# Two transformer blocks on one core: where sigmoids, up-tile copies, PSUM banks and sums of squares are placed

## Time and profile before

| | |
|---|---|
| time, median of three runs | 955.78 us (955.57 to 955.84) |
| the profiled execution: its time, its span | 955.88 us, 954.7 us |
| TensorE matmul, weight load busy | 926.0 us (97%), 887.9 us (93%) |
| VectorE, ScalarE, GpSimd busy | 664.5 us (70%), 480.2 us (50%), 68.3 us (7%) |
| DMA | 154.73 MB, mean 162 GB/s |
| instructions recorded | 17976, of which 7290 matmuls |

### The profile page before, as it was taken

How to read it: one execution, slowest core, us unless ns; L and a number is a source line. 1 busy time by engine, 2 the same in 40 slices (tenths; PEclk the granted TensorE clock), 3 DMA queues, 4 the chain that set the end, 5 groups by cost and what they waited for, 6 DMA issues and landing times.

```text
span 954.7 us, 17976 instructions
## 1 busy us (share of the span) xinstructions
PE 926.0 (97%) x7290; PEld 887.9 (93%) x7290; DVE 664.5 (70%) x1160; ACT 480.2 (50%) x856; POOL 68.3 (7%) x125
## 2 busy tenths in 40 slices
PE   8999999999899999999999999997999999999997
PEld 6899988999899999997999978996999999999997
DVE  6654575668878877787889966665657666665566
ACT  5355445545655555465456634443436544444456
POOL 5122000231000000000000100000102000000001
PEclk9999999999999999999999999998999999999999
DMA  7643443544465555654544552545556565665541
GB/s 273 185 148 110 137 137 120 148 145 147 141 199 178 179 193 179 184 177 148 177 133 134 154 178 74 170 154 155 179 164 198 176 196 181 180 191 184 186 144 45
DMA packets 43170, 154.73 MB, mean 162 GB/s; under 512 B 4688, under 2 KB 6224, under 8 KB 42960
## 3 DMA queue, kind: packets, MB, share of 16 engines
q1 hardware_dynamic: 43088, 153.59, 51.3%
HBM read 152.52 MB, written 1.05 MB: 161 GB/s over the span
## 4 chain that ended last, share of the span: by engine, by line
PE 81%; DVE 9%; ACT 5%; issue 4%; POOL 1%; DMA 1%; SPq 0%; DVEq 0%; ACTq 0%
PE bank L242 80%; DVE wl L1263 3%; ACT wh L825 2%; POOL tmpb L1860 1%; DMA raw<-in_wts 1%; DVE wh L1259 1%; ACT work L1060 1%; DVE work L1618 0%; DVE work L1616 0%; DVE tmpb L1803 0%; DVE tmpb L1454 0%; DVE xnl L1267 0%; DVE tmpb L1455 0%; ACT tmpb L1076 0%; DVE work L1599 0%
## 5 line engine op out<-in xcount | busy, mean ns | idle before, releaser
L1263 DVE TENSOR_TENSOR wl<-raw,wh 128x1024 fp32r<-128x1024 f32 x285 | 351.5, 1237 | 131.4 <-ACT wh L825 129.6
L825 ACT ACTIVATE wh<-raw 128x1024 fp32r<-128x1024 f32 x250 | 262.3, 1052 | 134.1 <-PE bank L242 132.9
L242 PE MATMUL bank<-a2h,wh 128*128 128x256 f32 x880 | 251.5, 287 | 6.2 <-DVE wl L1263 3.8
L242 PE MATMUL bank<-a2h,wl 128*128 128x256 f32 x880 | 247.8, 282 | 0.0
L242 PE MATMUL bank<-a2l,wh 128*128 128x256 f32 x880 | 245.6, 282 | 0.0
L242 PE MATMUL bank<-a1h,wh 128*128 128x258 f32 (+1 forms) x800 | 227.9, 287 | 6.1 <-issue 5.9
L242 PE MATMUL bank<-a1h,wl 128*128 128x258 f32 (+1 forms) x800 | 225.2, 283 | 0.0
L242 PE MATMUL bank<-a1l,wh 128*128 128x258 f32 (+1 forms) x800 | 220.6, 282 | 0.0
L242 PEld LDWEIGHTS bank<-a2h,wh 128*128 128x128 f32 x880 | 166.4, 189 | 10.3 <-issue 5.7
L242 PEld LDWEIGHTS bank<-a2h,wl 128*128 128x128 f32 x880 | 166.4, 189 | 0.0
L242 PEld LDWEIGHTS bank<-a2l,wh 128*128 128x128 f32 x880 | 165.5, 189 | 0.2
(11 more groups left out here) (229 smaller groups left out, 1022.4 us busy)
## 6 DMA issues: line engine op xcount, KB each, us to landing
raw<-in_wts SPq DMA_DIRECT2D x285, 512.0 KB, 3.6
csb<-in_cst SPq DMA_DIRECT2D x1, 1428.0 KB, 10.7
hT<-in_xT SPq DMA_DIRECT2D x2, 544.0 KB, 4.3
out<-va SPq DMA_DIRECT2D x2, 512.0 KB, 2.9
qk<-in_pT SPq DMA_DIRECT2D x1, 256.0 KB, 3.8
gr<-in_lamv SPq DMA_DIRECT2D x1, 128.0 KB, 10.6
ccol<-in_fcst SPq DMA_DIRECT2D x1, 126.0 KB, 4.7
```

The source lines that it names most:

```text
L242: return e.matmul(o, lhsT, rhs, start=start, stop=stop, skip_group_check=True)
L825: e.activation(wh[:, i % NHL, :], raw[:, i % NRAW, :], ACT.Copy).then_inc(s_hi, 1)
L1263: e.tensor_tensor(lo, src, hi.bitcast(F32), ALU.subtract).then_inc(s_lo, 1)
```

## The change

Seven edits. ScalarE applies the sigmoid of gate tile t - 1, no longer t, in iteration t. In feed-forward 1 VectorE copies up tile n + 1 right after the taps of tile n, so ahead of the product. In mix 1 `mix_hi` and `mix_lo` lag by two tiles. In w_out 1 tile 6 gets bank 6 and tile 7 bank 4. The second round of retention values goes to banks 2 and 5. VectorE adds retention's two squares of a head before one matmul sums them, and adds the eight squares ahead of the gate norm to two.

```diff
-        MIX_BANK = (0, 1, 2, 3, 4, 5, 4, 5)
+        MIX_BANK = (0, 1, 2, 3, 4, 5, 6, 4)
+        VR_BANK = ((0, 1), (2, 5))
@@ tensor_engine
-                elif m >= 6:
-                    e.wait_ge(s_mt, m - 1)
+                elif m == 7:
+                    e.wait_ge(s_mt, 5)
...
-            warm(12, 6)
+            e.wait_ge(s_mt, 6)
+            warm(12, 5)
@@ ret_sum(h)
-                e.wait_ge(s_rq, 2 * h + 2)
-                if h == 0:
-                    e.wait_ge(s_dc, 8)
-                else:
+                e.wait_ge(s_rqa, h + 1)
+                if h:
                     e.wait_ge(s_rln, h)
-                for j in range(2):
-                    t = mm(bank[B_T2][:, 0:S], ones, qk[:, 8 + 2 * h + j, 0:S], j == 0, j == 1)
-                t.then_inc(s_rss, 1)
+                mm(bank[B_T2][:, 0:S], ones, qk[:, 8 + 2 * h, 0:S], True, True).then_inc(s_rss, 1)
@@ retention values
-                for c in range(2):
-                    e.wait_ge(*ev2(21 + 2 * r + c))
-                values(B_VR + 4 * r, [(24 + 2 * r + c) % 3 for c in range(2)], (0, 128), N_IN2,
+                if r == 0:
+                    e.wait_ge(*ev2(22))
+                else:
+                    e.wait_ge(*ev2(23))
+                    e.wait_ge(s_dc, 8)
+                values(B_VR + 4 * r, VR_BANK[r], (0, 128), N_IN2,
@@ gate tiles
-            def gate_sum(k):
-                if k == 0:
-                    e.wait_ge(s_x3, 6)
-                e.wait_ge(s_sqa, 44 + k + 1)
-                t = mm(bank[B_GS][:, 0:S], ones, qk[:, k, 0:S], k == 0, k == KT - 1)
...
+            def gate_sum():
+                e.wait_ge(s_x3, 6)
+                e.wait_ge(s_sq, 14 + 3)
+                mm(bank[B_GS][:, 0:S], ones, qk[:, 3, 0:S], True, False)
+                e.wait_ge(s_sq, 14 + 6)
+                mm(bank[B_GS][:, 0:S], ones, qk[:, 7, 0:S], False, True).then_inc(s_sum, 1)
...
-            group(B_GP, ..., A1[0], A1[1], after=gate_sum)
+            group(B_GP, ..., A1[0], A1[1])
...
-                tile(B_GP + m, bank[GB[m % 3]][:, 0:S], A1[0], A1[1], range(KT)).then_inc(s_blk, 1)
+                tile(B_GP + m, bank[GB[m % 3]][:, 0:S], A1[0], A1[1], range(KT),
+                     mid=gate_sum if m == 2 else None).then_inc(s_blk, 1)
@@ scalar_engine, mix 1 (vector_engine: the same with mix_lo)
-                if m:
-                    mix_hi(N_MIX1, m - 1, xnh[:, :, 0:LQ])
+                if m >= 2:
+                    mix_hi(N_MIX1, m - 2, xnh[:, :, 0:LQ])
+            mix_hi(N_MIX1, 6, xnh[:, :, 0:LQ])
@@ scalar_engine, proj2
+            def gate2_sigmoid(m):
+                e.wait_ge(*ev2(36 + m))
+                e.activation(GATE2(m), GATE2(m), ACT.Sigmoid).then_inc(s_gs, 1)
...
                 hi_to(i + 4)
                 pump2(p)
-                if t >= 36:
-                    e.wait_ge(*ev2(t))
-                    e.activation(GATE2(t - 36), GATE2(t - 36), ACT.Sigmoid).then_inc(s_gs, 1)
+                if t > 36:
+                    gate2_sigmoid(t - 37)
                 pump2(p + 1)
...
             for m in range(8):
                 hi_to(B_BR + 2 * m + 5)
+                if m == 0:
+                    gate2_sigmoid(15)
@@ vector_engine, feed-forward 1
+            def up_out(n):
+                i = up1(n // 2, n % 2)
+                e.wait_ge(s_blk, i + 1)
...
+                e.tensor_tensor(work[:, n % 8, 0:LQ], bank[n % 4][:, 0:LQ], rb[:, 0, 0:LQ], ALU.mult).then_inc(s_u, 1)
+                lo_to(B_FF + 6 if n == 1 else i + 4)
+
+            up_out(0)
...
-                        e.tensor_tensor(u, bank[(2 * j + half) % 4][:, 0:LQ], rb[:, 0, 0:LQ], ALU.mult).then_inc(s_u, 1)
-                        lo_to(B_FF + 6 if (j, half) == (0, 1) else i + 4)
...
                         e.scalar_tensor_tensor(x, u[:, 0:S], ccol[:, c:c + 1], x, ALU.mult, ALU.add).then_inc(s_cb, 1)
+                        if n + 1 < 2 * FF1:
+                            up_out(n + 1)
@@ vector_engine, retention: ret_add(h) at RET_AT[h] + 3
+            def ret_add(h):
+                a = qk[:, 8 + 2 * h, 0:S]
+                e.wait_ge(s_rq, 2 * h + 2)
+                e.tensor_tensor(a, a, qk[:, 9 + 2 * h, 0:S], ALU.add).then_inc(s_rqa, 1)
@@ vector_engine, ahead of the gate tiles
+            def square_pair(a, b, squares):
+                e.wait_ge(s_sqa, squares)
+                e.wait_ge(s_sq, pairs["n"])
+                e.tensor_tensor(qk[:, a, 0:S], qk[:, a, 0:S], qk[:, b, 0:S], ALU.add).then_inc(s_sq, 1)
+                pairs["n"] += 1
...
+                if m in (3, 5, 7):
+                    square_pair(m - 2, m - 3, 44 + m - 1)
+                if m == 5:
+                    square_pair(3, 1, 44 + 4)
             lo_to(B_GP + 4)
+            square_pair(7, 6, 44 + 8)
+            square_pair(7, 5, 44 + 8)
```

More of the change, by code:

```diff
@@ L195, in program @@
             sem(f"s_{n}") for n in ("rz", "rp", "ro", "ry", "rq", "rss", "rln", "rrs", "rn"))
-        s_pt = sem("s_pt")
+        s_rqa, s_pt = sem("s_rqa"), sem("s_pt")
         s_sg, s_sm, s_sh, s_yr = sem("s_sg"), sem("s_sm"), sem("s_sh"), sem("s_yr")
@@ L769, in tensor_engine @@
                 ple(B_PLE1, m, m - 4)
-            def gate_sum(k):
-                if k == 0:
-                    e.wait_ge(s_x3, 6)
-                e.wait_ge(s_sqa, 44 + k + 1)
-                t = mm(bank[B_GS][:, 0:S], ones, qk[:, k, 0:S], k == 0, k == KT - 1)
-                if k == KT - 1:
-                    t.then_inc(s_sum, 1)
+            def gate_sum():
[4 more added lines that the diff above has]
+                mm(bank[B_GS][:, 0:S], ones, qk[:, 7, 0:S], False, True).then_inc(s_sum, 1)
             e.wait_ge(s_x3, 4)
-            group(B_GP, [bank[b][:, 0:S] for b in GB[0:2]], 0, S, N_GATE, A1[0], A1[1], after=gate_sum)
+            group(B_GP, [bank[b][:, 0:S] for b in GB[0:2]], 0, S, N_GATE, A1[0], A1[1])
             def turn_out(m):
@@ L1465, in vector_engine @@
                 lo_to(B_WO + m + 4)
-                if m:
-                    mix_lo(N_MIX1, m - 1, xnh[:, :, 0:LQ], xnl[:, :, 0:LQ])
+                if m >= 2:
+                    mix_lo(N_MIX1, m - 2, xnh[:, :, 0:LQ], xnl[:, :, 0:LQ])
                 e.wait_ge(s_blk, B_WO + m + 1)
@@ L1470, in vector_engine @@
                 mix(N_MIX1, m, LQ, bank[(2 * m + 1) % 8][:, 0:LQ], bank[2 * m % 8][:, 0:LQ])
+            mix_lo(N_MIX1, 6, xnh[:, :, 0:LQ], xnl[:, :, 0:LQ])
             mix_lo(N_MIX1, 7, xnh[:, :, 0:LQ], xnl[:, :, 0:LQ])
@@ L1519, in z_lo @@
                 low(a2l[:, zi, :], src, a2h[:, zi, :]).then_inc(s_zl, 1)
+            def up_out(n):
+                i = up1(n // 2, n % 2)
+                e.wait_ge(s_blk, i + 1)
+                if n == 0:
+                    e.wait_ge(s_rs, 3)
+                if n >= 8:
+                    e.wait_ge(s_cb, n - 7)
+                e.tensor_tensor(work[:, n % 8, 0:LQ], bank[n % 4][:, 0:LQ], rb[:, 0, 0:LQ], ALU.mult).then_inc(s_u, 1)
+                lo_to(B_FF + 6 if n == 1 else i + 4)
+            up_out(0)
             for j in range(FF1 + LAG1):
@@ L1523, in vector_engine @@
                     for half in range(2):
-                        i = up1(j, half)
+                        n = 2 * j + half
                         c = COL_CONV + 4 * (half * FF1 + j)
[L1526 to L1531, removed]
-                        e.tensor_tensor(u, bank[(2 * j + half) % 4][:, 0:LQ], rb[:, 0, 0:LQ], ALU.mult).then_inc(s_u, 1)
-                        lo_to(B_FF + 6 if (j, half) == (0, 1) else i + 4)
-                        e.wait_ge(s_cv, 2 * j + half + 1)
+                        x, u = tmpb[:, n % 6, 0:S], work[:, n % 8, 0:LQ]
+                        e.wait_ge(s_cv, n + 1)
                         e.scalar_tensor_tensor(x, u[:, 1:1 + S], ccol[:, c + 1:c + 2], x, ALU.mult, ALU.add).then_inc(s_ca, 1)
@@ L1537, in vector_engine @@
                             z_lo(j, (j - 1) % 4, tmpb[:, (2 * j - 1) % 6, 0:S])
-                        e.wait_ge(s_ca, 2 * j + half + 1)
+                        e.wait_ge(s_ca, n + 1)
                         e.scalar_tensor_tensor(x, u[:, 0:S], ccol[:, c:c + 1], x, ALU.mult, ALU.add).then_inc(s_cb, 1)
+                        if n + 1 < 2 * FF1:
+                            up_out(n + 1)
                     g, v = tmpb[:, 2 * j % 6, 0:S], tmpb[:, (2 * j + 1) % 6, 0:S]
@@ L1703, in pump2 @@
                         ret_copy(h)
+                    elif j == 3:
+                        ret_add(h)
                     elif j == 5:
@@ L1734, in vector_engine @@
                     pump2(48 + 8 * r + 2 * q + 1)
-                values2_out(B_VR + 4 * r, lambda c: va[:, 4 + 2 * r + c, :], [(24 + 2 * r + c) % 3 for c in range(2)], s_evD, r_tok)
+                values2_out(B_VR + 4 * r, lambda c: va[:, 4 + 2 * r + c, :], VR_BANK[r], s_evD, r_tok)
             for t in range(28, 52):
@@ L1778, in vector_engine @@
                     lo_to(down2(j - LAG2) + 4)
+            pairs = {"n": 14}
```

(2 more changed lines are left out.)

## The result

The changed kernel took 937.85 us (median of four runs, 937.65 to 940.0) against 955.75 us (955.57 to 955.84): ratio 0.9818, 95% interval 0.9801 to 0.9835. It is faster by 17.9 us; forecast were 19.2 us (936.6 us), range 934.5 to 941.5. Its profiled execution is the slowest of the four, 940.0 us for a span of 938.7 us.

The account below looks back on a forecast made before the run. TensorE, with a matmul in flight for 97% of the span, was taken as the bound. Gains of 10.5 + 2.0 + 0.8 + 0.75 + 1.4 + 1.6 + 1.7 + 0.5 = 19.25 us from 955.88 gave 936.6 us, range 934.5 to 941.5.

Parts of the forecast that it names:

- The reading of the hole as a wait: Gate stage, ahead of the branches: TensorE's 5.9 us idle is waiting for late VectorE; 8.9 us gained, 10.5 with clock.
- Mix 1 and bank 6: Mix 1's lag of two gains 2.0 us; bank 6 for w_out 1 tile 6 gains 0.8 us.
- Value banks and retention's squares: Second value round no longer waits for copies, 1.6 us; four fewer matmuls in retention, 1.7 us.
- Gate squares: Gate norm: sums 3.5 us shorter, but the end hangs on the VectorE and ScalarE chain, so 0.5 us gained.
- Up tiles ahead of the product: Start of feed-forward 1: earlier copy cuts TensorE's 2.87 us idle to 2.1, 0.75 us gained, plus 1.4 from the clock.
- It fits, so 0: Feed-forward 1 steady state: VectorE's 1.7 to 2.4 us behind the copy's wait fits in 2.85 us, no cost.
- is needed six tiles later: Feed-forward 1: the gelu product, now behind a wait for TensorE's up tile, is needed only six tiles later.
- The clock at 250 us: After feed-forward 1's first hole, shortened to 2.1 us, the granted clock stays up: 1.4 us gained, bounds 0 and 1.4.
- The slower rival: Feed-forward 1: each down block's low half comes too late, about 20 times, 970 us; chance 0.03.
- the forecast's 1.6: Branches after the 5.9 us hole: 19 matmuls ran 4 us at low clock, 2.3 at full, so 1.6 us gained.
- my reasoning from two rows: Clock fell after 2.87 us idle, not after 1.42; 2.1 lies nearer to what kept it, so it stays up.

Follow-up runs that it names:

- the last pair's order: Changed kernel with, for the last pair alone, the copy of up tile 42 behind the product of pair 20 again: 938.55 us.
- gate sigmoids alone: Kernel before with only the gate sigmoids a tile behind: 945.18 us, ratio 0.9887.
- up tiles undone: Changed kernel with the up tiles' copies back behind the gelu product: 938.42 us.
- mix 1 alone: Kernel before with only the lag of two in mix 1 and bank 6 for w_out 1 tile 6: 953.01 us, ratio 0.9981.
- values alone: Kernel before with only value banks 2 and 5 and retention's squares added on VectorE: 953.48 us, ratio 0.9977.
- up tiles alone: Kernel before with only the up tiles' copies ahead of the product: 957.19 us, ratio 1.0019.
- gate squares undone: Changed kernel with the eight sums of the gate norm back on TensorE alone: 939.5 us.
- changed kernel again: The changed kernel run once more with no edit, for a second profile and the clock: 939.42 us.
- gate sigmoids undone: Changed kernel with the sigmoid of gate tile t put back in iteration t: 949.38 us.
- lag of three: Changed kernel with feed-forward 1 down tiles three pairs behind the up tiles, not two: 938.27 us.
- the two versions without it: Changed kernel with down tiles three pairs behind and early weight halves: 935.06 us; with more early halves and the last square on VectorE besides: 932.54 us.

## Why the prediction was right, and where it was off

The median, 937.85, is 1.2 us above the forecast of 936.6 and inside the range; so is that of the second set, 939.42 against 955.42 for the kernel before, 16.0 less. The mechanisms of the large terms were right. One term was luck and one was missing, and they nearly cancel.

- **The reading of the hole as a wait**, right: removed and put back at 5.90 us by one edit. Size 8.9, measured 8.92 and 8.93; with the clock behind it 10.5, measured 10.5 in the profiles of the edit alone (8.93 + 1.60) and 10.4 in time.
- **Mix 1 and bank 6**, right: 2.8, measured 2.9. No run has one without the other. GpSimd and VectorE held each other up (a subtraction of 1.22 us took up to 1.82), and TensorE did not wait for it.
- **Value banks and retention's squares**, right: 1.6 + 1.7, measured 1.66 and, with the last sum, 1.74; 3.4 in all.
- **Gate squares**, right in the size (0.5; measured 0.4) and in the form: the new wait of 0.7 us at tile 2, and an end that hangs on VectorE and ScalarE. How the wait ahead of the output would grow (0.97 to 1.40 us) it did not say.
- **Up tiles ahead of the product**: the first hole right (2.1; 2.09). The step that failed is "It fits, so 0". I had compared VectorE's 1.7 to 2.4 us with TensorE's 2.85 us for the weight halves, and said of the product that it "is needed six tiles later". That holds while up tiles stand between; at the end of the stage none do. The last down tiles follow each other, ScalarE has a table load of 1.28 us in that chain, and the chain had no slack: what the edit put behind the copy's wait came out as 1.30 us at one place. That is the whole difference between 19.25 and 18.21, within 0.3. With 0.77 us gained at the first hole, this edit was a loss of 0.5 us, not the gain of 0.75 + 1.4 that the sum has.
- **The clock at 250 us**: counted as a gain of 1.4 because the hole got shorter. The size of a fall was right (1.5 measured), the reason was not, as the last section shows: with the longer hole the clock stayed up in three profiles of five. The forecast was made against an execution in which it fell. In the first set of the changed kernel the mean clock (0.998, 0.998, 0.998, and 0.997 in the profiled one, which fell) says that it stayed up in three of four executions, in the second set that it did in at least one of four. That the median of the first set has this gain is luck; without it the edits are worth about 16.7 us (18.21 - 1.5), and that is nearer to the 16.0 of the second set.
- The slower rival's mechanism (low halves regularly late in feed-forward 1) did not come: no wait for `wl` between 260 and 410 us. But its place, what stands behind the copy's wait, is where the one late half came from.

## What to carry to other kernels

When an instruction is moved ahead of others and it waits for another engine, list what now stands behind that wait and check it at the stage's last iteration as well as in the steady state, where later tiles hide it. Subtract stages between two profiles by the first matmul of each stage; here that settles 0.1 us in most stages, where two medians of the same kernel differ by 1.6 us. Check on a stage that no edit touches, or on a third profile, how far it repeats: the last 6 us here differ by 0.6 us between profiles for no reason but the clock, as much as the term that was to be measured there. A hole labelled "issue" that closes just behind another engine's instruction is a wait like any other.

## What the runs showed of the hardware

The granted clock went with the time in steps. Of 19 executions of the kernel before in one set, the 8 with a mean clock of 0.995 took 954.07 to 954.5 us, the 7 with 0.993 took 955.45 to 956.99, the 4 with 0.991 or 0.990 took 957.08 to 957.82. In the changed kernel's second set 937.8 went with 0.998, and 939.1 to 940.2 with 0.996 or 0.995.

The mean clock does not tell where it was low, though. In every profile it is also low in the last 3 to 7 us, where TensorE has little to do, and how early that begins varies. The profiled execution of the last pair's order has a mean of 0.996, but kept 1.00 behind its hole of 2.09 us (first row); what it has less than the 0.998 of the changed kernel's second profile (last row) lies at the end:

```profile
252.00:256.00 4.00, 4.00 (x36) 4.00 (x35) 3.96 (x8) 3.50 (x6) 0.00 (x0) 1.00 0.63 212
928.00:932.00 4.00, 2.42 (x14) 1.78 (x13) 0.92 (x3) 3.20 (x8) 0.00 (x0) 0.75 0.00 0
```

```profile
928.00:932.00 4.00, 2.12 (x18) 1.64 (x16) 1.07 (x4) 3.61 (x9) 0.00 (x0) 1.00 0.00 0
```

So 0.996 does not prove a fall at 250 us; 0.998, in the one profile that has it, goes with none. A fall there costs what rows show: with the same hole of 2.09 us the two profiles of the changed kernel took 175.70 us (248.71 to 424.41, clock fallen) and 174.19 us.

```profile
249.70:253.10 3.40, 3.40 (x18) 3.40 (x17) 3.31 (x8) 2.11 (x4) 0.00 (x0) 0.50 0.66 222
```

```profile
249.00:253.00 4.00, 4.00 (x36) 4.00 (x36) 3.91 (x8) 2.67 (x5) 0.00 (x0) 1.00 0.77 236
```

All these are windows (stretch, us, busy time with counts by engine, granted clock, DMA share, GB/s). The two just above are of the first and the second profile of the changed kernel: 18 matmuls in 3.4 us at 0.50, the 1.2 GHz level, against 36 in 4 us at 1.00. And the length of a hole of 2 to 3 us does not decide it. Behind the hole of 2.87 us the clock fell in 2 profiles (before, gate sigmoids alone) and not in 3 (up tiles undone, mix 1 alone, values alone); behind that of 2.09 us it fell in 3 (changed kernel, up tiles alone, gate squares undone) and not in 4 (changed kernel again, gate sigmoids undone, the last pair's order, lag of three). In the 5.9 us it fell in all 5, but not at the same point, and that sets the price: where the low clock began 3.3 to 3.5 us before TensorE started again (before, up tiles alone, values alone), the branches took 62.28 to 62.37 us; where it began only 0.7 or 0.8 us before (gate sigmoids undone, mix 1 alone), 63.46 and 63.50; with no fall 60.77. So the forecast's 1.6 was the cheap case of 1.5 to 2.7. In the shorter holes the fall began between 0.7 us before the restart and 1.5 us behind it. With the hole of 2.86 us and no fall (up tiles undone), then with one of 2.87 us and a fall (gate sigmoids alone) that lasted from 250.7 to 257.5 us, twice as long as the others, and cost 2.7 us (175.59 for the rest of feed-forward 1 against 172.86 to 172.95 with no fall):

```profile
248.50:252.00 3.50, 3.50 (x29) 3.50 (x30) 3.36 (x8) 1.86 (x3) 0.00 (x0) 1.00 0.46 150
```

```profile
251.40:257.00 5.60, 5.60 (x26) 5.60 (x27) 5.46 (x11) 3.21 (x6) 0.00 (x0) 0.50 0.65 182
```

The Trainium skill, page "TensorE: Matmul & The Clock Gate", section "Part 1: The HAM clock gate (the "warmup" mystery)", says that the activity is watched in a window that runs freely, and that the number of slow matmuls at a kernel's start therefore varies between runs of the same kernel. It says this of the start, not of a hole in the middle; the counts above would fit such a window, but no run here shows it.

So my reasoning from two rows (2.87 lost it, 1.42 kept it, 2.1 is nearer to 1.42) had no ground. What decides in such a hole is open. The safe gain is to have no such hole: in the two versions without it the executions lie within 0.3 us (four) and 0.4 us (five).
